# Reading the moving rows of a two-layer decoder trunk from the last token, with the two weight tiles of a unit interleaved column by column

## The reference

```python
for l in range(2):
    h = h + 0.5 * rmsnorm(swiglu(rmsnorm(h, g[0]), ffn_w_in[l, 0], ffn_w_out[l, 0]), g[1])
    hn = rmsnorm(h, g[2])
    u_pool, q, k, v, gate_pool, gate_attn = split(hn @ w_in[l])
    y_pool = pool_mixer(u_pool, pool_w_grp[l], pool_scale[l], w_pool_proj[l])
    y_attn = swa_attention(q, k, v, sinks[l]) @ w_attn_proj[l]
    merged = sigmoid(gate_pool) * y_pool + sigmoid(gate_attn) * y_attn
    h = h + rmsnorm(merged @ w_o[l], g[3])
    h = h + 0.5 * rmsnorm(swiglu(rmsnorm(h, g[4]), ffn_w_in[l, 1], ffn_w_out[l, 1]), g[5])
return h[:, 16:]
```

## Time and profile before

| | |
|---|---|
| median of 3 runs | 1175.15 us (1174.69 to 1175.27) |
| the profiled execution's own time | 1174.66 us |
| its span, first to last instruction | 1172.8 us |
| TensorE matmul busy | 1163.3 us (99%), 9269 matmuls |
| TensorE weight load busy | 1136.1 us (97%), 9269 loads |
| VectorE busy | 733.0 us (62%) |
| ScalarE busy | 554.8 us (47%) |
| GpSimd busy | 430.8 us (37%) |
| mean granted TensorE clock | 0.999 |
| DMA | 197.58 MB, mean 168 GB/s |

### The profile page before, as it was taken

The page is one execution under the profiler, slowest core; times in us unless marked ns, Lnnn a source line. Parts: engine busy times, 40 slices in busy tenths (PEclk is TensorE's granted clock), DMA queues, the critical chain, the costliest instruction groups (busy, mean ns, idle before and its releaser), DMA issues.

```text
span 1172.8 us, 23880 instructions
## 1 busy us (share of the span) xinstructions
PE 1163.3 (99%) x9269; PEld 1136.1 (97%) x9269; DVE 733.0 (62%) x1145; ACT 554.8 (47%) x818; POOL 430.8 (37%) x486
## 2 busy tenths in 40 slices
PE   9999999999999999999999999999999999999997
PEld 8999999999999999999999999999999999999986
DVE  7655546968666965544586555459676769755542
ACT  7433335637554653333454333356375556533441
POOL 1945500007211286551109555000082122955500
PEclk9999999999999999999999999999999999999999
DMA  9754458372365365535646543573723744654550
GB/s 295 257 179 156 147 179 233 123 232 72 91 190 170 108 216 179 170 121 196 205 134 216 179 157 133 189 226 109 247 82 93 213 145 144 216 179 161 189 170 36
DMA packets 197934, 197.58 MB, mean 168 GB/s; under 512 B 4448, under 2 KB 191200, under 8 KB 197856
## 3 DMA queue, kind: packets, MB, share of 16 engines
q1 hardware_dynamic: 197712, 196.44, 52.4%
q10 hardware_dynamic: 144, 0.05, 0.0%
HBM read 195.43 MB, written 1.05 MB: 168 GB/s over the span
## 4 chain that ended last, share of the span: by engine, by line
PE 92%; issue 3%; DVE 2%; ACT 1%; POOL 0%; DMA 0%; SPq 0%; DVEq 0%; ACTq 0%; POOLq 0%
PE bank L553 27%; PE bank L554 27%; PE bank L555 27%; PE bank L811 2%; PE bank L809 2%; PE bank L810 2%; DVE w_lo L1326 1%; PE bank L898 1%; PE bank L893 1%; PE bank L852 1%; PE bank L588 1%; PE bank L587 1%; PE bank L863 1%; PE bank L615 0%; PE bank L855 0%
## 5 line engine op out<-in xcount | busy, mean ns | idle before, releaser
L553 PE MATMUL bank<-x_hi,w_hi 128*128 128x272 f32 (+1 forms) x1991 | 573.8, 288 | 0.8 <-DVE w_lo L1732 0.8
L554 PE MATMUL bank<-x_lo,w_hi 128*128 128x272 f32 (+1 forms) x1991 | 568.4, 285 | 0.0
L555 PE MATMUL bank<-x_hi,w_lo 128*128 128x272 f32 (+1 forms) x1991 | 568.3, 285 | 0.0
L1009 ACT ACTIVATE w_hi<-raw 128x2048 fp32r<-128x2048 f32 (+3 forms) x201 | 339.0, 1693 | 401.7 <-PE bank L555 388.9
L1326 DVE TENSOR_TENSOR w_lo<-raw,w_hi 128x2048 fp32r<-128x2048 f32 (+3 forms) x203 | 420.3, 2076 | 143.2 <-ACT w_hi L1009 142.9
L553 PEld LDWEIGHTS bank<-x_hi,w_hi 128*128 128x128 f32 x1991 | 377.1, 189 | 1.9 <-issue 0.7
L554 PEld LDWEIGHTS bank<-x_lo,w_hi 128*128 128x128 f32 x1991 | 377.2, 189 | 0.3
L555 PEld LDWEIGHTS bank<-x_hi,w_lo 128*128 128x128 f32 x1991 | 377.1, 189 | 0.0
L1943 POOL TENSOR_TENSOR hid_hi<-silu,up_r 128x272 f32 x88 | 142.5, 1619 | 149.8 <-DVE up_r L1520 144.3
L555 PE MATMUL bank<-hid_hi,w_lo 128*128 128x272 f32 x528 | 151.3, 287 | 0.0
L553 PE MATMUL bank<-hid_hi,w_hi 128*128 128x272 f32 x528 | 151.3, 286 | 0.0
(11 more groups left out here) (219 smaller groups left out, 1323.5 us busy)
## 6 DMA issues: line engine op xcount, KB each, us to landing
raw<-in_ffn_w_in SPq DMA_DIRECT2D x84, 1024.0 KB, 5.0
raw<-in_w_in SPq DMA_DIRECT2D x24, 1024.0 KB, 5.6
raw<-in_ffn_w_out SPq DMA_DIRECT2D x24, 768.0 KB, 4.2
raw<-in_ffn_w_out SPq DMA_DIRECT2D x24, 640.0 KB, 3.9
raw<-in_ffn_w_out SPq DMA_DIRECT2D x10, 1024.0 KB, 5.0
raw<-in_w_in SPq DMA_DIRECT2D x16, 512.0 KB, 5.2
raw<-in_w_attn_proj SPq DMA_DIRECT2D x32, 256.0 KB, 4.3
raw<-in_w_o SPq DMA_DIRECT2D x8, 1024.0 KB, 5.6
```

The costliest lines, as they stand in the source:

```text
L553: pe.matmul(ps[:, t0:T], w[0], a_hi[:, t0:T], start=start, stop=False)
L554: pe.matmul(ps[:, t0:T], w[0], a_lo[:, t0:T], start=False, stop=False)
L555: return pe.matmul(ps[:, t0:T], w[1], a_hi[:, t0:T], start=False, stop=stop)
L1009: last = act.activation(hi, w, ACT.Copy)
```

## The change

The moving operand of every large product, and with it the PSUM rows it is written to, is read with a step of minus one, from the last token (or, in `end_out`, the last weight column) to the first. The two tiles of a unit are interleaved: output column j of tile 0 stands at 2j and that of tile 1 at 2j + 1 of the unit's 256, so `weights` takes every second column. The host lays the weights out that way (`in_pairs`), and puts the columns of q in the order of the units (`by_units`), so the units of q are loaded with one DMA and split in one piece. The weights of the last FFN out keep their order. In the diff below the same edit at other call sites is left out.

```diff
 def unit_dmas(u):
-    return 2 if U_Q <= u < U_POOL else 4 if U_AP <= u < U_WO else 1
+    return 4 if U_AP <= u < U_WO else 1
...
-            if not U_Q <= u < U_POOL:
-                cuts = [n // pieces * i for i in range(pieces + 1)]
-                return [(raw[:, s, a:b], w_hi[:, s, a:b], w_lo[:, s, a:b]) for a, b in zip(cuts, cuts[1:])]
-            from_raw = raw[:, s, :].rearrange("p (k s t c) -> p t k s c", s=2, t=2, c=DH)
-            to_hi, to_lo = (w[:, s, :].rearrange("p (k t s c) -> p t k s c", s=2, t=2, c=DH) for w in (w_hi, w_lo))
-            k = KD * 2 // max(pieces, 2)
-            return [(from_raw[:, t, a:a + k], to_hi[:, t, a:a + k], to_lo[:, t, a:a + k])
-                    for t in range(2) for a in range(0, KD, k)]
+            cuts = [n // pieces * i for i in range(pieces + 1)]
+            return [(raw[:, s, a:b], w_hi[:, s, a:b], w_lo[:, s, a:b]) for a, b in zip(cuts, cuts[1:])]
...
-                    if U_Q <= u < U_POOL:
-
-                        c = q0 + (8 * ((u - U_Q) // 2) + 2 * ((u - U_Q) % 2)) * DH
-                        to = raw[:, u % RING, :].rearrange("p (k s c) -> p k s c", s=2, c=P)
-                        for side in range(2):
-                            load(u, w[:, :, c + side * 4 * DH:c + side * 4 * DH + P], to[:, :, side, :])
-                    else:
-                        c = (k0 if u == U_K else v0 if u == U_V else (u - U_POOL) * UW if u < U_GATE
-                             else g0 + (u - U_GATE) * UW)
-                        load(u, w[:, :, c:c + UW])
+                    c = (k0 if u == U_K else v0 if u == U_V else q0 + (u - U_Q) * UW if u < U_POOL
+                         else (u - U_POOL) * UW if u < U_GATE else g0 + (u - U_GATE) * UW)
+                    load(u, w[:, :, c:c + UW])
...
-                return [w[:, s, k * UW + mt * P:k * UW + (mt + 1) * P] for w in (w_hi, w_lo)]
+                return [w[:, s, k * UW + mt:(k + 1) * UW:2] for w in (w_hi, w_lo)]
+
+            def backwards(ps, w, a, first, end, start, stop):
+
+
+                return pe.matmul(ps[:, first:end][:, ::-1], w, a[:, first:end][:, ::-1], start=start, stop=stop)
 
             def products(ps, w, a_hi, a_lo, start, stop, t0):
 
-                pe.matmul(ps[:, t0:T], w[0], a_hi[:, t0:T], start=start, stop=False)
-                pe.matmul(ps[:, t0:T], w[0], a_lo[:, t0:T], start=False, stop=False)
-                return pe.matmul(ps[:, t0:T], w[1], a_hi[:, t0:T], start=False, stop=stop)
+                backwards(ps, w[0], a_hi, t0, T, start, False)
+                backwards(ps, w[0], a_lo, t0, T, False, False)
+                return backwards(ps, w[1], a_hi, t0, T, False, stop)
...
-                            pe.matmul(ps[:, :], hid_hi[:, k, cols], w[0], start=k == 0, stop=False)
-                            pe.matmul(ps[:, :], hid_hi[:, k, cols], w[1], start=False, stop=False)
-                            return pe.matmul(ps[:, :], hid_lo[:, k, cols], w[0], start=False, stop=k == KF - 1)
+                            backwards(ps, hid_hi[:, k, cols], w[0], 0, HALF_D, k == 0, False)
+                            backwards(ps, hid_hi[:, k, cols], w[1], 0, HALF_D, False, False)
+                            return backwards(ps, hid_lo[:, k, cols], w[0], 0, HALF_D, False, k == KF - 1)
...
+def in_pairs(w):
+
+
+    tiles = w.reshape(*w.shape[:-1], w.shape[-1] // UW, 2, P)
+    return np.ascontiguousarray(np.swapaxes(tiles, -1, -2)).reshape(w.shape)
+
+
+def by_units(w):
+
+
+    q = w[..., POOL_DIM:POOL_DIM + Q_DIM]
+    heads = q.reshape(*q.shape[:-1], 2, 2, 2, 2, DH)
+    units = np.swapaxes(np.moveaxis(heads, -4, -3), -3, -2)
+    return np.concatenate([w[..., :POOL_DIM], units.reshape(q.shape), w[..., POOL_DIM + Q_DIM:]], axis=-1)
```

More of the change, by code:

```diff
@@ L585, in high @@
                     w = weights(u + c // 2, k, c % 2)
-                    cols = slice(max(starts[c // 2], first), end)
-                    pe.matmul(bank[banks[c]][:, cols], w[0], x_hi[:, k, cols], start=k == 0 and c >= CUT_TILES, stop=False)
-                    pe.matmul(bank[banks[c]][:, cols], w[1], x_hi[:, k, cols], start=False, stop=False)
+                    first = max(starts[c // 2], first)
+                    backwards(bank[banks[c]], w[0], x_hi[:, k, :], first, end, k == 0 and c >= CUT_TILES, False)
+                    backwards(bank[banks[c]], w[1], x_hi[:, k, :], first, end, False, False)
                 for k in range(KD):
@@ L614, in deep_three @@
                         if k < HIGH_FIRST:
-                            pe.matmul(bank[banks[c]][:, t0:T], w[0], x_lo[:, k, t0:T], start=False, stop=False)
+                            backwards(bank[banks[c]], w[0], x_lo[:, k, :], t0, T, False, False)
                             continue
@@ L623, in product @@
                 def product(c, k, low_weights, operand, start=False, stop=False):
-                    return pe.matmul(bank[OPEN_BANKS[c]][:, 0:T], weights(c // 2, k, c % 2)[low_weights], operand[:, k, :],
-                                     start=start, stop=stop)
+                    return backwards(bank[OPEN_BANKS[c]], weights(c // 2, k, c % 2)[low_weights], operand[:, k, :], 0, T,
+                                     start, stop)
                 pe.wait_ge(xhi_ready, 1)
@@ L2049, in laid_out @@
         return geometry_table()
+    if name in ("ffn_w_in", "w_in", "w_pool_proj", "w_attn_proj", "w_o"):
+        return in_pairs(by_units(np.asarray(inputs[name])) if name == "w_in" else np.asarray(inputs[name]))
+    if name == "ffn_w_out":
+        w = np.asarray(inputs[name])
+        laid = in_pairs(w)
+        laid[DEPTH - 1, 1] = w[DEPTH - 1, 1]
+        return laid
     if name == "x_columns":
```

## The result

The changed kernel takes 1195.46 us (median of 4 runs, 1194.98 to 1195.78) against 1174.95 us of the kernel before beside it: a ratio of 1.0174, with a 95% interval of 1.0156 to 1.0192. It is 20.5 us slower where 50 us faster was forecast.

What follows compares the result with a forecast made beforehand. TensorE's pairs times their distance were taken as the bound; 36.5 us (272 columns) plus 16.6 us (256 columns) less 3 us given back is 50 us, from 1174.66 to 1124.6, so 1125 us; range 1095 to 1192 us.

Steps and rivals of the forecast that it cites:

- What bounds the kernel: On TensorE: the end is set by the number of weight load and matmul pairs times their start-to-start distance.
- That the excess hangs on addresses: In TensorE's pairs: the 10.0 to 13.3 ns above the columns' time vary with where operands lie in SBUF.
- I take that 40% of the excess stays: In the large products: 272 columns go from 123.3 to 117.3 ns, 256 from 120.0 to 112.0; 36.5 and 16.6 us less.
- the floor of 110 ns: For 256-column pairs: lower bound on the new distance, a weight load of 128 columns, from transposes 0.11 us apart.
- The second rival: At the rows' start address: the good match is lost, 1.9 ns more on 8167 pairs, 15.5 us, 1191 us; chance 0.13.
- The third rival: In weight loads: a step of two covers twice the bytes and doubles the excess, 88.5 us more, 1264 us; chance 0.11.
- Half rate: In reversed matmuls: backward read or PSUM write takes each column twice as long, 844 us more, 2019 us; chance 0.06.
- The 512 columns: In the last FFN out, only the moving side reversed: between 3.5 us less and as much more, taken as nothing.
- Given back: In the attention stages: VectorE now and then late for a faster TensorE, 3 us lost, bounded by 0 and 9 us.
- units of q: In eight units of q: one ScalarE copy less each, 1.4 us in all, hidden under TensorE's stream, taken as nothing.

Runs made afterwards that it cites:

- the probe: Kernel before with 42, then 50 groups of 24 matmul pairs behind its last result, varying columns, step, direction and offset; about 125 us above 1175, then about 1330 us.
- the last version: Kernel before with x rows from layer 1's mixer on placed so 256 columns are read from 240 above a multiple of 256; 1165.35 us (0.9918).

## Why the prediction was wrong

**What bounds the kernel: right.** The end moved by the number of pairs times their distance, to within 0.2 us; the two other terms that the traces show, 0.8 and 0.9 us, have opposite signs.

**That the excess hangs on addresses: right**, and shown now without any other engine: one move of the rows by 64 bytes was worth 16 us.

**"I take that 40% of the excess stays": wrong, and this is the step that failed.** The excess over the columns' own time was to fall from 10.0 to 4.0 ns with 272 columns; in the kernel it rose to 13.4. With 256 columns it was to fall from 13.3 to 5.3 ns, and it stayed at 13.3. The step rested on the two reads keeping out of each other's way once both go backwards at one speed. What the probe has for that is little: with step two and backwards the distance of 272 columns no longer cares for six of eight offsets, but with 256 columns it still goes from 117.8 to 120.1 ns over the four offsets tried. The level at which 272 columns settle is 124.4 ns, an excess of 11.1 ns. That is above the 10.0 ns which the kernel before had, so none of the eight offsets tried had anything to win for 272 columns. In which order a load goes through its columns, on which the argument hung, no run shows.

**Where the numbers of that step came from.** For 272 columns I chose near the lower end by an argument on bytes in a given time, with no row at that end. For 256 columns the floor of 110 ns was that of loads with a step of one, while the edit gives the load a step of two: such a load alone comes every 118 ns in the probes, so 112.0 ns was out of reach. The 0.11 us of the earlier trace rows is a rounded 117 ns; of the 92 distances between such pairs in the trace two are 112 ns, and the median is 118. That 256 and 512 columns had the same excess of 13.3 ns was chance: by offset alone 256 columns range from 113.4 to 120.0 ns.

**The place.** START 64, the best offset of the old order, is one of the two that fall out of that level in the new one, at 126.3 to 126.5. The second rival named the lost match of addresses, gave it 0.13 and priced it at 1191 us: 1.9 ns on all 8167 pairs. It was 3.3 ns on 5785 of them and nothing or nearly nothing on the 256 columns and on o. That the two products lie 4 us apart is luck, as the 1.9 ns were o's distance with the old reads.

**The third rival**, that the excess doubles with the ground that a load covers, is wrong in size, and its sign hangs on the place: the step of two alone adds 4.2 ns forwards at 64 in the kernel, and at 128 takes 1.0 ns away in the probe. **Half rate** is wrong as well. The Trainium skill (Advanced Engine Details and Errata, Memory Cachelines) has PSUM patterns that aren't contiguous slow a matmul; 123.5 against 123.4 ns for reversed PSUM rows says that falling order is not such a pattern. Its rule that two hits on an SBUF line are enough is a little off for a load: 118 ns with a step of two against 112 with one.

**The 512 columns.** I took nothing within 3.5 us either way; it was 1.6 us more, all of it from the reversal. Reversed reads and reversed PSUM rows were told apart with 272 columns only, so which of them costs here is not shown.

**Given back, units of q.** The 3 us for VectorE never arose, as TensorE did not get faster; in the last version, with layer 1 faster, one new wait for VectorE of 0.7 us arose, as said above. The units of q are worth nothing that can be measured, as said.

## What to carry to other kernels

When TensorE is busy all the time, count its pairs in a stretch and take the columns' own time off: what is left over (10 to 13 ns of 120 here) is a quantity to tune, and the placement of the rows is its cheapest handle. Order of reading, step and placement act together, so a placement tuned for one order has to be searched again for another; a ladder of some fifty short groups behind the kernel's last result reads all of it in one run. What it promises has to be confirmed in the kernel: 240 kept its 113 ns there, and 64 came at 118 in the FFN. A step of two in the stationary operand makes the load itself about 6 ns longer (118 against 112) and shouldn't be expected to come free.

## What was not expected of the hardware

- Two pairs with equal work differ by up to 6.6 ns in 120 by the addresses of their operands alone: 256 columns take 113.4 ns at 240 and 120.0 ns at 224.
- In the kernel a reversed row of 512 columns costs 6 ns more than a plain one (233.4 against 227.3). In the probe a step of two in the weights brings a plain one (229.6) to the same 233 ns, and both together cost no more than either.
- The step of two and the reversal don't add up: 4.2 and 1.6 ns alone, 3.3 together, for 272 columns at 64.
